# Prompt attention: a minimum becomes two relus, and high and low parts change engines

## The reference, cut to what matters

```python
DIL_PATTERNS = ((128, 1), (512, 4), (2048, 16))

def fox_prompt(q, k, v, logf):                       # full causal attention
    s = jnp.einsum('bqhd,bkhd->bhqk', qb, k) * scale + cb[..., :, None] - c[..., None, :]
    p, _ = softmax_stats(s, kpos[None, :] <= qpos[:, None])
    return jnp.einsum('bhqk,bkhd->bqhd', p, v)

def merge_groups(outs, lses):                        # dilated windows
    o = jnp.stack(outs, 0)
    a = jax.nn.softmax(jnp.stack(lses, 0), axis=0)
    return jnp.einsum('gbsh,gbshd->bshd', a, o)
```

## Time and profile before

| | |
|---|---|
| time, 3 runs | 1769.53, 1770.48 (median), 1772.14 us |
| the profiled execution | 1768.47 us, of it 1766.7 us span |
| mean granted TensorE clock | 0.982 |
| TensorE busy | 1684.6 us (95% of the span) |
| VectorE busy | 1086.5 us (61%) |
| ScalarE busy | 908.8 us (51%) |
| GpSimd busy | 850.5 us (48%) |
| `attend_prompt` | 1074.7 to 1239.8 us: 165 us, 9% of the span |

### The profile page before, as it was taken

One profiled execution on the slowest core, in us unless ns is written; L12 is line 12 of the kernel. 1 busy time (PEld: TensorE's weight loads), 2 busy tenths in 40 slices (PEclk: granted clock), 3 DMA queues, 4 the chain that ended last, 5 costly groups with the idle time before them and its releaser, 6 DMA issues. The chain is left out here.

```text
span 1766.7 us, 31754 instructions
## 1 busy us (share of the span) xinstructions
PE 1684.6 (95%) x10669; PEld 1512.9 (86%) x10669; DVE 1086.5 (61%) x2256; ACT 908.8 (51%) x1593; POOL 850.5 (48%) x530
## 2 busy tenths in 40 slices
PE   6999999999889999999999977888899999999998
PEld 5888888899879899899998956887888989898997
DVE  5747466522388888888888886997634514234251
ACT  5444344433358888888878885766224312222230
POOL 1515243300228878788787755674333334343432
PEclk9999999999899999999999997999899999999999
DMA  7385575545799999999999984441745575756662
GB/s 227 102 304 209 207 270 205 186 134 152 224 310 353 345 351 351 354 351 345 346 360 346 353 274 141 147 135 30 251 169 214 215 284 214 278 221 261 238 261 78
DMA packets 181993, 432.66 MB, mean 245 GB/s; under 512 B 29009, under 2 KB 71946, under 8 KB 180434
## 3 DMA queue, kind: packets, MB, share of 16 engines
q1 hardware_dynamic: 177906, 420.21, 67.4%
q10 hardware_dynamic: 2560, 8.39, 1.6%
q0 software_dynamic: 1376, 2.10, 0.5%
HBM read 398.23 MB, written 119.70 MB: 293 GB/s over the span
## 5 line engine op out<-in xcount | busy, mean ns | idle before, releaser
L1143 POOL TENSOR_TENSOR vv_lo<-v_raw,vv_hi 128x1024 fp32r<-128x1024 f32 x178 | 401.5, 2260 | 148.0 <-ACT vv_hi L1239 146.0
L2241 POOL TENSOR_TENSOR w_lo<-w_raw,w_hi 128x2048 fp32r<-128x2048 f32 x39 | 180.2, 4619 | 320.8 <-ACT w_hi L2255 320.8
L1231 ACT ACTIVATE kt_hi<-ktp 128x1024 fp32r<-128x1024 f32 (+1 forms) x192 | 186.2, 970 | 94.4 <-PE ktp L1432 93.6
L1266 DVE TENSOR_TENSOR kt_lo<-ktp,kt_hi 128x1024 fp32r<-128x1024 f32 (+1 forms) x192 | 221.0, 1151 | 9.1 <-ACT kt_hi L1231 7.3
L1446 PE MATMUL s_ps<-kt_hi,q_st 128*128 128x256 f32 (+3 forms) x768 | 205.6, 301 | 0.8 <-DVE mx_parts L1316 0.4
L1432 PE MATMUL ktp<-ident,k_raw 128*128 128x128 f32 x1440 | 192.9, 276 | 8.6 <-DVEq L1257 3.8
L1432 PEld LDWEIGHTS ktp<-ident,k_raw 128*128 128x128 f32 x1440 | 169.3, 142 | 33.0 <-issue 5.6
L750 PE MATMUL acc<-w_hi,xn_hi 128*128 128x512 f32 x480 | 192.4, 401 | 2.9 <-POOL w_lo L374 2.9
L1239 ACT ACTIVATE vv_hi<-v_raw 128x1024 fp32r<-128x1024 f32 (+1 forms) x192 | 191.4, 997 | 4.7 <-PE o_ps L1462 4.1
L1446 PE MATMUL s_ps<-kt_lo,q_st 128*128 128x256 f32 (+3 forms) x768 | 190.6, 282 | 0.0
L750 PE MATMUL acc<-w_lo,xn_hi 128*128 128x512 f32 x480 | 187.9, 391 | 0.0
(11 more groups left out here) (271 smaller groups left out, 3938.5 us busy)
## 6 DMA issues: line engine op xcount, KB each, us to landing
k_raw<-in_cache_fox_k SPq DMA_DIRECT2D x256, 256.0 KB, 4.9
v_raw<-in_cache_fox_v SPq DMA_DIRECT2D x256, 256.0 KB, 4.6
out_win_kv_sample<-in_cache_win_kv SPq DMA_DIRECT2D x32, 2040.0 KB, 9.7
w_raw<-in_w_in SPq DMA_DIRECT2D x32, 1024.0 KB, 5.8
k_raw<-in_cache_win_kv SPq DMA_DIRECT2D x40, 512.0 KB, 9.2
v_raw<-in_cache_win_kv SPq DMA_DIRECT2D x40, 512.0 KB, 8.5
w_raw<-in_w_up SPq DMA_DIRECT2D x16, 1024.0 KB, 5.4
w_raw<-in_w_down SPq DMA_DIRECT2D x16, 1024.0 KB, 5.1
```

The source lines that it names most:

```text
L1143: gp.tensor_tensor(vv_lo[:, slot, 0:tiles, :], v_raw[:, i % RAW_RING, 0:tiles, :], vv_hi[:, slot, 0:tiles, :].bitcast(F32), ALU.subtract). ...
L1231: act.activation(kt_hi[:, slot, :, 0:n], ktp[:, i % 2, :, 0:n], ACT.Copy).then_inc(k_hi, 1)
L1266: ve.tensor_tensor(kt_lo[:, slot, :, 0:n], ktp[:, i % 2, :, 0:n], kt_hi[:, slot, :, 0:n].bitcast(F32), ALU.subtract).then_inc(k_lo, 1)
L2241: gp.tensor_tensor(w_lo[slot][:], w_raw[:, slot, :], w_hi[slot][:].bitcast(F32), ALU.subtract).then_inc(slab_lo_done, 1)
```

## The change

The minimum is gone. GpSimd now makes one difference `apart` = near - spread of the two log-sums; ScalarE takes relu(apart) and relu(-apart), and the exponential with scale -1 of both. This gives the same pair of weights. The copy of the spread output out of PSUM goes from ScalarE to VectorE. All high parts of queries are ScalarE's now, and the low parts of the upper head's queries (pieces 8 to 11) GpSimd's, each directly behind a lower piece (4 to 7, `PARTNER`), with a wait for its own completion behind each of the two. The mask falls two steps later. The first pair's pieces 4 to 7 are split in the end of `attend_sample` too. Of the first weights, ScalarE makes the high part in step 55 and GpSimd the low part in step 56.

The diff, without the allocation of tiles and semaphores, and without the bodies of functions that only disappear:

```diff
-PIECE_STEP = (0, 0, 1, 1, 2, 2, 3, 4, 5, 5, 6, 7)
-EARLY_PIECES = 4
-EARLY_STEP = (0, 1, 2, 3)
-FIRST_PIECE_STEP = (0, 0, 1, 2, 3, 4, 5, 6)
+PIECE_STEP = (0, 0, 1, 1, 2, 4, 5, 7, 3, 4, 5, 7)
+PARTNER = (4, 5, 6, 7)
+EARLY_STEP = (0, 1, 2, 3, 4, 5, 6, 7)
+FIRST_PIECE_STEP = (1, 2, 4, 6)
...
+HI_OF = {None: "k_hi", 0: "q_hi", 1: "upper_hi"}
...
                         piece_lo(gp, ahead, p, j)
+                        if j in PARTNER:
+                            n = PARTNER.index(j)
+                            gp.wait_ge(part_lo, LOWER_PIECES * p + j + 1)
+                            piece_lo(gp, ahead, p, LOWER_PIECES + n)
+                            gp.wait_ge(upper_lo, UPPER_PIECES * p + n + 1)
...
-                near, spread = near_stat[:, h % STATS, 0, :], stat[:, h % STATS, SPREAD, 0, :]
-                gp.wait_ge(least_done, h + 1)
-                after(gp, shares_done, h)
-                gp.tensor_tensor(gap[:, 0, :], least[:], near, ALU.subtract)
-                gp.tensor_tensor(gap[:, 1, :], least[:], spread, ALU.subtract).then_inc(gap_done, 1)
+                gp.wait_ge(near_in, 16 * (h + 1))
+                after(gp, gap_sides, h)
+                gp.tensor_tensor(apart[:], near_stat[:, h % STATS, 0, :], stat[:, h % STATS, SPREAD, 0, :], ALU.subtract).then_inc(apart_done, 1)
...
+            def weights_lo(h, i):
+                if h == HEADS - 1 and i == 0:
+                    gp.wait_ge(lead_w, 1)
+                    gp.tensor_tensor(w0_lo[:], w_raw[:, 0], w0_hi[:].bitcast(F32), ALU.subtract)
+
...
-            straight(HEADS, STEPS, *(first_lo(j) for j in range(EARLY_PIECES, LOWER_PIECES)), (1, mask_diagonals), *(pieces_lo(j) for j in range(LOWER_PIECES)),
-                     *(values_lo(w, first) for w in range(SETS) for first in (True, False)), (13, gaps), (14, weights), (15, divide), (23, scale))
+            straight(HEADS, STEPS, (3, mask_diagonals), *(pieces_lo(j) for j in range(LOWER_PIECES)),
+                     *(values_lo(w, first) for w in range(SETS) for first in (True, False)), (13, differ), (14, weights), (15, divide), (23, scale), (7, weights_lo))
...
+            def pieces_hi(j):
                 def stage(h, i):
                     p, (hh, s) = h // 2 + 1, PIECES[j]
-                    if i == 0 and h % 2 == 0 and p < PAIRS and hh is None:
-                        act.wait_ge(raw_in[raw_part(1, s)], 16 * (p + 1))
+                    if i or h % 2 or p == PAIRS:
+                        return
+                    act.wait_ge(raw_in[raw_part(hh is None, s)], 16 * (p + 1))
+                    if hh is None:
                         after(act, scored, 2 * STEPS * (p - 1))
-                        act.activation(part_of(ahead, p, 0, hh, s), raw_cols(ahead, hh, s), ACT.Copy).then_inc(k_hi, 1)
+                    else:
+                        act.wait_ge(scored, STEPS * (2 * p - 2 + hh) + {2: 2, 3: 2, 1: 4, 0: STEPS}[s])
+                    act.activation(part_of(ahead, p, 0, hh, s), raw_cols(ahead, hh, s), ACT.Copy).then_inc(ahead[HI_OF[hh]], 1)
 
                 return PIECES_BEHIND + PIECE_STEP[j], stage
...
-                    act.wait_ge(gap_done, h + 1)
-                    act.activation(gap[:], gap[:], ACT.Exp).then_inc(gap_exp, 1)
-
-                act.activation(spread_of(p)[rows], o_ps[rows, SPREAD, :], ACT.Copy).then_inc(copied[SPREAD], 1)
+                    act.wait_ge(apart_done, h + 1)
+                    after(act, shares_done, h)
+                    act.activation(gap[:, 0, :], apart[:], ACT.Relu)
+                    act.activation(gap[:, 1, :], apart[:], ACT.Relu, scale=-1.0).then_inc(gap_sides, 1)
+                    act.wait_ge(gap_sides, h + 1)
+                    act.activation(gap[:], gap[:], ACT.Exp, scale=-1.0).then_inc(gap_exp, 1)
+
+            def split_weights(h, i):
+                if h == HEADS - 1 and i == 0:
+                    act.wait_ge(slab_loaded[0], 32)
+                    act.wait_ge(part_lo, LOWER_PIECES * PAIRS)
+                    act.wait_ge(upper_lo, UPPER_PIECES * PAIRS)
+                    act.activation(w0_hi[:], w_raw[:, 0], ACT.Copy).then_inc(lead_w, 1)
 
             def split_lead(h, i):
                 if h < HEADS - 1 or i < STEPS - 1:
                     return
-                act.wait_ge(slab_loaded[0], 32)
                 act.wait_ge(scored, STEPS * HEADS)
-                act.activation(w0_hi[:], w_raw[:, 0], ACT.Copy).then_inc(lead_w, 1)
...
-            straight(HEADS, STEPS, *(first_hi(j) for j in range(EARLY_PIECES, len(PIECES))),
-                     (EXP_P_BEHIND, exponentials), (TURN_BEHIND, turns_hi), (14, gap_exponentials), (10, copy_spread),
-                     *(keys_hi(j) for j in range(len(PIECES))), *(values_hi(w, first) for w in range(SETS) for first in (True, False)),
-                     (TURN_BEHIND + 1, split_lead))
+            straight(HEADS, STEPS, *(first_hi(j) for j in range(LOWER_PIECES, len(PIECES))),
+                     (EXP_P_BEHIND, exponentials), (TURN_BEHIND, turns_hi), (14, gap_exponentials),
+                     *(pieces_hi(j) for j in range(len(PIECES))), *(values_hi(w, first) for w in range(SETS) for first in (True, False)),
+                     (6, split_weights), (TURN_BEHIND + 5, split_lead))
...
-                        ve.tensor_copy(part_of(ahead, p, 0, hh, s), raw_cols(ahead, hh, s)).then_inc(q_hi, 1)
...
-                        piece_lo(ve, ahead, p, j)
...
+            def first_upper_lo(j):
...
+                        piece_lo(ve, ahead, 0, j)
...
-                    ve.tensor_tensor(least[:], near_stat[:, h % STATS, 0, :], stat[:, h % STATS, SPREAD, 0, :], ALU.min).then_inc(least_done, 1)
...
+            def copy_spread(h, i):
+                if i == 0:
+                    after(ve, scaled, h // 2 - 1)
+                    ve.wait_ge(weighed[SPREAD], len(SPREAD_JOBS) * (h + 1))
+                    ve.tensor_copy(spread_of(h // 2)[rows_of(h)], o_ps[rows_of(h), SPREAD, :]).then_inc(copied[SPREAD], 1)
+
...
-            straight(HEADS, STEPS, *(clear_rest(n) for n in range(3)), (KEEP_BEHIND, keep), (18, keep_shares), (LOW_BEHIND, turns_lo), (9, invert_far), (12, least_of_both), (15, invert_whole), (12, copy_near), (14, copy_far), *(queries_hi(j) for j in range(len(PIECES))),
-                     *(upper_queries_lo(j, first) for j in range(LOWER_PIECES, len(PIECES)) for first in (True, False)))
-            ve.wait_ge(lead_w, 1)
-            ve.tensor_tensor(w0_lo[:], w_raw[:, 0], w0_hi[:].bitcast(F32), ALU.subtract)
+            straight(HEADS, STEPS, *(clear_rest(n) for n in range(3)), (KEEP_BEHIND, keep), (18, keep_shares), (LOW_BEHIND, turns_lo), (9, invert_far), (15, invert_whole), (10, copy_spread), (12, copy_near), (14, copy_far),
+                     *(first_upper_lo(j) for j in range(LOWER_PIECES, len(PIECES))))
```

More of the change, by code:

```diff
@@ L1172, in first_pair @@
                 return FIRST_PIECES_BEHIND + EARLY_STEP[j] + 1, stage
-            straight(DEC_BATCH, PER_BATCH, (0, per_batch), (EXP_BEHIND, values_lo), *(first_pair(j) for j in range(EARLY_PIECES)))
+            straight(DEC_BATCH, PER_BATCH, (0, per_batch), (EXP_BEHIND, values_lo), *(first_pair(j) for j in range(LOWER_PIECES)))
         @block.scalar
@@ L1251, in _ @@
             straight(DEC_BATCH, PER_BATCH, (OUT_BEHIND, out_low), (EXP_BEHIND, exponentials), (0, keys_hi), (0, load_bias), (0, load_first_bias), (EXP_BEHIND, values_hi),
-                     *(first_pair(j) for j in range(EARLY_PIECES)))
+                     *(first_pair(j) for j in range(LOWER_PIECES)))
         @block.vector
@@ L1516, in piece_hi @@
     act.wait_ge(ahead["raw_in"][raw_part(hh is None, s)], 16)
-    act.activation(part_of(ahead, 0, 0, hh, s), raw_cols(ahead, hh, s), ACT.Copy).then_inc(ahead["k_hi" if hh is None else "q_hi"], 1)
+    act.activation(part_of(ahead, 0, 0, hh, s), raw_cols(ahead, hh, s), ACT.Copy).then_inc(ahead[HI_OF[hh]], 1)
 def piece_lo(eng, ahead, p, j):
     hh, s = PIECES[j]
-    of_keys = hh is None
-    eng.wait_ge(ahead["k_hi" if of_keys else "q_hi"], sum((h is None) == of_keys for h, _ in PIECES) * p + sum((h is None) == of_keys for h, _ in PIECES[:j + 1]))
+    eng.wait_ge(ahead[HI_OF[hh]], sum(h == hh for h, _ in PIECES) * p + sum(h == hh for h, _ in PIECES[:j + 1]))
     done = ahead["upper_lo" if hh == 1 else "part_lo"]
@@ L1569, in early_prompt @@
                  bias=at("bias3", [P, 2, FOX_TILES * P], F32, offset=small_at + 4 * (4 * P)))
-    for name in ("q_hi", "k_hi", "part_lo", "upper_lo", "zeroed", "masks_in", "shares_sent", "share_in"):
+    for name in ("q_hi", "k_hi", "part_lo", "upper_hi", "upper_lo", "zeroed", "masks_in", "shares_sent", "share_in"):
         ahead[name] = nc.alloc_semaphore(f"ahead_{name}")
@@ L1608, in attend_prompt @@
         share_rows = sb("share_rows3", [P, 2, P])
-        least, whole, r_whole = (sb(n, [P, RESIDUES]) for n in ("least3", "whole3", "r_whole3"))
```

(30 more changed lines are left out.)

18 lines of the change are left out of this document (4 added, 14 removed).

## The result

The change makes the kernel slower: 1775.92 us (median of 9 runs, 1772.59 to 1780.2) against 1769.59 us of the kernel before in the same rounds, a ratio of 1.0039 (95% interval 1.003 to 1.0048). The forecast was 1769.0, the range 1761.0 to 1775.5. The profiled execution has a span of 1770.7 us, 4.0 more than before. At 1772.59 us it is the fastest of the nine, so what its profile shows is somewhat less than what the medians differ by (6.3 us).

A forecast was written before the change was run, and what follows sets the result against it. VectorE was taken to bound the kernel, GpSimd's queue after the change. Start −1.7, pairs −2.5, +1.1 and −0.7, end +2.3 gave −1.5 us: profiled 1768.47 to 1767.0, median 2.0 above, 1769.0; range 1761.0 to 1775.5.

The forecast's parts named there:

- A: The forecast itself: GpSimd's queue takes VectorE's place as the bound, −1.5 us in all, 1769.0 us; chance 0.44.
- VectorE bounds before; 43.6 us leave it: Prompt's attention: VectorE is the fullest engine, and three groups of 43.6 us in 114 us leave it.
- GpSimd's row of 28.3 us and the mask behind it: Second pair: GpSimd's queued work sums to 28.3 us, its mask ending 29.7 us after TensorE's step 23 starts.
- T34 to T37 in 6.56 us: TensorE's step 34 start to step 37 start takes 6.56 us as before, plus about 0.5 us of slow clock.
- T34 under T23 + 28: Refuting sign: TensorE's step 34 starting less than 28 us after step 23 would mean GpSimd's queue is hidden.
- GpSimd's busy time per pair: Sign in the changed profile: GpSimd's busy time rises to 32 us or more of 37 per pair.
- The first pair: TensorE's step 9 to step 23: 36.5 us against 39.0, −2.5 us, with 0.8 us of slow clock included.
- The start: Start of the stage: barrier 2.9 us later, TensorE's 4.72 us wait gone, mask's bias late next; step 9 starts 1.7 us earlier.
- The end: End of the stage: first weights' high part in step 55 and GpSimd's 4.62 us low part cost +2.3 us.
- C: Slower rival: TensorE's stalls at the mask bring the 1.2 GHz clock, +2.5 us a window, 1776 us; chance 0.20.
- 1.8 us of slow clock: Slow clock included in the forecast over three pairs; the lighter rival left it out for −1.8 us.

The follow-up runs named there:

- a_mask1_up_dve: Changed kernel with the mask in step 1 of a head and the upper head's query low parts back on VectorE: 1753.17 us, ratio 0.9919.
- b_relu: Kernel before with only the minimum replaced by GpSimd's difference and two relus on ScalarE: 1768.12 us, ratio 1.0003.
- a_mask2: Changed kernel with the mask one step earlier, in step 2 of a head instead of 3: 1758.14 us, ratio 0.9943.
- b_mask3: Kernel before with only the mask moved, to step 3 of a head instead of 1: 1764.72 us, ratio 0.9983.
- a_up_dve: Changed kernel with the upper head's query low parts back on VectorE, the mask left in step 3: 1760.74 us, ratio 0.9964.
- a_fill: Changed kernel with ten unused matmuls ahead of the scores in steps 34 and 48, the mask still late: 1763.42 us, ratio 0.9978.
- b_early: Kernel before with only the first pair's pieces 4 to 7 moved into the end of the samples' stage: 1768.25 us, ratio 1.0004.
- a_wlo_dve: Changed kernel with the low part of the first weights back on VectorE, last of all: 1773.4 us, ratio 1.0036.

## Why the prediction was wrong

A's mechanism, GpSimd's queue and the late mask, was right. What A put behind the stall, 0.5 us of slow clock, was wrong by ten times.

- *VectorE bounds before; 43.6 us leave it.* That they leave is shown: 106 to 66 us. That VectorE held the pairs is in part argued: with the mask in step 1 and the casts gone from it, pairs fell to 32.3 us (a_mask1_up_dve), but no run moves the casts alone. And "a blocked instruction goes, its time goes" does not hold one by one: b_relu removed 12.79 us of minima, and 7.7 came back in the casts.
- *GpSimd's row of 28.3 us and the mask behind it.* Right in its terms: the row took 28.0 us from T23 + 1.5, the mask ended at T23 + 29.6 (forecast 29.7), and the turn followed at T23 + 31.2. a_mask2 shows that the order of the row decides. b_mask3 shows that the late mask costs nothing with eight pieces and the old pairs, a_up_dve that it costs 2.1 us a pair with eight pieces and shorter pairs, at a clock of 1.00.
- *T34 to T37 in 6.56 us, "with about 0.5 us of slow clock".* This is the step that failed. From the turn to T37 the forecast leaves 6.5 us; it took 10.7. The term carried the price of the slow clock as 0.5 us a pair; a_fill measured 4.8 and 5.4. The earlier trace rows had shown such a stretch behind 2.60 us of idle time, and the window around it gives its length, 6.9 us at 0.50:

```profile
1194.00:1202.00 8.00, 7.60 (x36) 0.57 0.03 3
```

In these 6.9 us TensorE does what takes some 3.4 us at 1.00, so the price to be read there was about 3.4 us a stall (an estimate), seven times what I put in, and still short of the 4.8 and 5.4 that came with 13.7 us at 0.50. Why the stretch was twice as long in the changed kernel no run shows.

- *A sign set at the wrong place.* I had written that T34 under T23 + 28 would refute A; it was T23 + 27.9. The scores of step 34 go ahead of the stalled turn, so the mark was at the wrong instruction, while the turn was where I put it. (The terms for T34 add up to 29.7 + 1.3 − 0.6, T23 + 30.4, not 30.6, which changes nothing here.) By the same slip the stall's length, 2.47 us between these scores and the turn, stood nowhere in the forecast. GpSimd's busy time per pair was 30.4 and 31.9 us, not 32 or more; the pairs were 42 us long and not 37.
- *The first pair.* 34.6 us instead of 36.5. GpSimd's row began at T9 + 3.4 instead of 3.9 and took 17.8 us to the sum that VectorE inverts (forecast 17.9). The turn of the shares came 1.8 us behind it instead of 0.8, T23 only 11.7 us behind the turn instead of 13.1, and the 0.8 us of slow clock that I added were not there (1.00).
- *The start.* −1.9 against −1.7, with the mask's transfer late next (GpSimd waited 9.72 us for the bias). The stage began 1.9 us later and not 2.9 (TensorE's first scores at 1076.82, before at 1074.90); GpSimd's last piece ahead of the barrier ended at 1074.22 and not at 1076.6. b_early shows that by itself this gain goes at the second pair.
- *The end.* +1.6 against +2.3. The low part on GpSimd took 4.53 us ahead of shares and scaling, and 2.1 us of it show at the stage's end (a_wlo_dve).
- *The chances.* C's condition came true, the clock in two pairs, and its 1776 is the measured 1775.92 by luck: it is a middle between two sums, with 2.5 us a window (measured: 4.8 and 5.4, in two windows), up to +4 at the end (measured: +1.6), and the first pair's gain 1.9 us too small. C had 0.20 because I asked whether the clock would fall; but A itself forecast a new stall and should have carried the price. Without its 1.8 us of slow clock and with 3.4 us in each of two pairs, A's time is 1769.0 − 1.8 + 6.8 = 1774; with the 5 us that only the later runs show, 1777.

## What to carry to other kernels

When work is moved to an engine with room by its busy share, write out its queue between two points that the critical engine needs, and put what the critical engine waits for at the front: one number in the step of the mask decided between 0.4% slower and 0.6% faster. A forecast stall of TensorE is priced with the slow clock behind it: look how long the clock stayed at 0.50 behind the longest such stall in the same kernel, and put in half of that, knowing that it can be more. Here 6.9 us were on view before, and 13.7 came; the slow clock cost about twice the 2.7 us of the wait. Taking one instruction from a contended engine gained nothing while the contention stayed (b_relu).

## What the runs showed of the hardware

- The slow clock: idle stretches of 2.47 us (the changed kernel) and of 2.60 us (the kernel before, at 1194.40) were followed by 0.50, one of 2.48 us (a_up_dve) was not. The stretch at 0.50 lasted 13.7 us in the changed kernel and 6.9 in the kernel before. Ten unused matmuls, 2.5 us together, put into the stall saved some 5 us each time (a_fill).
- VectorE bore most of the contention with GpSimd. A low part took GpSimd 1.27 us in most places while VectorE's casts of 64x512 took 0.8 us on average in the kernel before and 1.15 in b_relu. The Trainium skill, "SBUF — State Buffer", section "Who interferes with whom", lets the order of issue decide who blocks; which of two instructions was issued first no row here shows. GpSimd's own instructions took longer in places too: the third of the scaling took 1.88 us at 1161.55 in the kernel before and 1.56 at 1155.84 in the changed one.
- A relu of 128x4 on ScalarE took 0.19 to 0.21 us, and those of a pair's first head hid behind GpSimd's pieces, as the prediction had them: its weights followed the piece before without waiting.
